# First modulation panels as TensorE's moving operand, slices dealt to four column groups, input loaded first, one block fewer

## The chip, the cores and the metric

The kernel runs on one core of one Trainium2 chip. The metric is the device time of one execution in microseconds, the median of the runs. Three runs of the kernel before gave 1554.28, 1550.50 and 1553.59 us, median 1553.59. The profile is of one further execution of 1552.17 us; the span that it shows, from the first to the last instruction, is 1550.4 us. TensorE is called PE in the rows, VectorE DVE, ScalarE ACT, GpSimd POOL, and SyncE, which starts the DMAs, SP.

## The reference, cut to what matters

Two transformer-like blocks run on 512 tokens of width 1024 in float32. Each starts from a modulation vector, a matrix-vector product; the change touches only the first one, its bias and the first norm behind it:

```python
c_act = jax.nn.silu(c)                        # c: 1 x 1024
mod = c_act @ ada_w[i] + ada_b[i]             # ada_w: 1024 x 6144
sh1, sc1, g1, sh2, sc2, g2 = split(mod, 6)
h = rms_norm(x, mix_pre_g[i]) * (1.0 + sc1) + sh1
y = hybrid_mixer(h, w_in[i], ...)             # projections, attention, 31-tap convolution
x = x + g1 * rms_norm(y, mix_post_g[i])
```

The first projection needs h, so it needs `sh1` and `sc1` in full, 2048 of the 6144 columns. `g1` (1024 columns) is needed only behind the mixer.

## The kernel before

Everything lies transposed: 128 partitions hold features, the free dimension holds the 512 tokens, and a tensor of width 1024 is KT = 8 such tiles. Weights come in panels of 1 MB (128 x 2048), loaded by SP into two `raw` slots. ScalarE rounds a panel to `whi` (`split_hi`, line 187), VectorE forms the rest `wlo` (`split_lo`, line 191), and TensorE makes three passes, `whi` with `hhi`, `whi` with `hlo`, `wlo` with `hhi`. `in_panel` (line 242) is 48 matmuls of 512 columns. TensorE, VectorE and ScalarE each work through a hand-written order; semaphores join them. SP loads panel c+2 once `lo_split` says that the slot is free.

**Modulation panels.** The modulation matrix is also cut into panels of 1 MB: panel c holds 1024 rows as eight slices of 128 partitions (index k) by 256 output columns. Panels 0 to 7 (ADA_OWN = 8) are `sh1` and `sc1`, panels 8 to 11 are `g1`. `first` has room for panels 0 to 7, `ada_raw` holds two more at a time.

**First block, lines 544 to 646.** SP loads the vectors, the constants, modulation panel 0, the input `x` (2 MB), modulation panels 1 to 6 with weight panel 0 behind the last, modulation panel 7, weight panel 1, modulation panels 8 and 9, and then, each behind a wait, modulation panels 10 and 11 and weight panels 2 and 3. Panels 0 to 9 are multiplied and summed off TensorE, by turns (string `BY`, line 528). For even c GpSimd multiplies the panel by the activated vector `cs` (line 586) and VectorE reduces over k (line 609); for odd c VectorE alone runs a chain of eight instructions (lines 615 and 619). TensorE then only sums over the partitions: per panel two matmuls with the 128x128 piece of `ada_acc` as weights and one column of ones as moving operand (line 642; line 215 for panels 8 and 9). The norm of x sits between: squares by ScalarE (line 573, three buffers), sums over the partitions by eight 512-column float32 matmuls with ones as weights (line 638), square root and reciprocal on 128x512. VectorE ends with `split_lo` for weight panels 0 and 1.

**Second block, lines 648 to 663.** `read_mod` (line 234) adds the bias, `coefs` (line 415) forms the factor, and then per tile k VectorE forms `h0` (line 430), ScalarE `hhi` (line 439), VectorE `hlo` (line 424), and TensorE runs the six matmuls of tile k of weight panel 0 (line 449). A block ends when all engines have ended in it.

**Third block, lines 739 on.** TensorE runs weight panels 1 to 6 (`in_panel`, after panel 2 also `small_projection`), VectorE and ScalarE take each result, and VectorE fills its time with the taps of the convolution (line 732; `DENSE_TAPS`, 11 after most panels). Then attention runs in 16 units n: `logits(n)` (lines 790 to 797) on TensorE, maximum (line 1104) on VectorE, exponential (line 1001) on ScalarE, with pieces of later projections between (line 843). `logits(0)` waits for `ncx` (line 1077 on VectorE), `logits(1)` for the exponential of unit 0. Before `logits(0)` and `logits(1)` stands `ada_direct` (line 219): modulation panels 10 and 11 multiplied on TensorE with the panel as weights, 16 float32 matmuls each with one moving column. GpSimd sums modulation panels 12 to 19 after the last tap.

**Helpers that the change newly uses.** `token_sums` (line 292) sums squares with four matmuls of 32 weight columns, each writing its own 32 partitions of one bank for its own 128 tokens; `token_std` and `token_rs` are the root and the reciprocal on 128x128; `spread` (line 312) brings the result back to 128x512 with four matmuls.

## Time and profile before

| what | value |
|---|---|
| median of the runs | 1553.59 us (1550.50 to 1554.28) |
| profiled execution, span | 1552.17 us, 1550.4 us |
| TensorE matmuls busy | 1390.1 us, 90% of the span |
| VectorE busy | 938.6 us, 61% |
| ScalarE, GpSimd busy | 549.5 us, 556.6 us |
| DMA | 181.04 MB, mean 117 GB/s |
| 0 to 60 us: TensorE, VectorE busy | 17.97 us, 44.18 us |
| 80 to 200 us: TensorE, VectorE busy | 115.92 us of 120, 100.58 us |

Times of rows are microseconds from the start of the span unless marked ns. A timeline row gives start, duration, engine, line, operation, output and inputs with shape, how many instructions were merged, and in brackets the idle time of the engine before it with what ended it. A float32 matmul shows as two records, and each record lasts longer than the step to the next one, since matmuls are pipelined. A wait for several semaphores is put down to the one that came last.

### The profile page before, as it was taken

How to read it: one execution, taken by the hardware profiler on the slowest of the kernel's cores; microseconds unless marked ns; L12 is line 12 of the kernel's file. 1: busy time of each engine (PE TensorE's matmuls, PEld its weight loads, DVE VectorE, ACT ScalarE, POOL GpSimd, SP SyncE). 2: the span in 40 equal slices, each digit the busy share in tenths (PEclk: the TensorE clock that was granted, in tenths of full speed). 3: DMA queues.
4: the chain of work that ended last, by engine and by line, in shares of the span. 5: the costliest groups of instructions: out<-in, count | busy, mean ns of one | idle time of the engine just before them, and what ended most of it. 6: DMA issues, size and time to landing. Idle time of an engine off the chain costs nothing. (4 is left out here: it accounts for less than half of the span.)

```text
span 1550.4 us, 18593 instructions
## 1 busy us (share of the span) xinstructions
PE 1390.1 (90%) x7392; PEld 1102.5 (71%) x7392; DVE 938.6 (61%) x1031; ACT 549.5 (35%) x697; POOL 556.6 (36%) x260
## 2 busy tenths in 40 slices
PE   3399987888999998999899979988699899999997
PEld 1378765667888887888678856765478689777775
DVE  6988775776656464323765646777893561355553
ACT  3122345533232222112354433344442342355541
POOL 3000004954987875999200003322300041122320
PEclk8599798988999999999699989999699899999998
DMA  9322211431454545454122233222313243111121
GB/s 389 114 82 77 87 55 58 155 118 77 171 210 173 205 157 195 163 189 190 55 112 90 100 97 109 93 86 70 120 39 104 104 162 109 55 55 55 55 82 55
DMA packets 41346, 181.04 MB, mean 117 GB/s; under 512 B 3392, under 2 KB 20160, under 8 KB 21312
## 3 DMA queue, kind: packets, MB, share of 16 engines
q1 hardware_dynamic: 41280, 180.12, 32.1%
q8 instruction: 46, 0.75, 0.2%
q14 instruction: 20, 0.16, 0.0%
HBM read 173.75 MB, written 6.36 MB: 116 GB/s over the span
## 5 line engine op out<-in xcount | busy, mean ns | idle before, releaser
L191 DVE TENSOR_TENSOR wlo<-raw,whi 128x2048 fp32r<-128x2048 f32 x95 | 264.5, 2785 | 180.9 <-ACT whi L187 178.1
L198 POOL TENSOR_TENSOR ada_raw<-ada_raw,cs 128x2048 f32<-128x2048 f32 x44 | 174.0, 3956 | 380.2 <-DVE cv L732 170.3
L253 PE MATMUL ps<-hhi,whi 128*128 128x512 f32 x640 | 251.8, 393 | 2.4 <-DVE wlo L191 0.8
L253 PE MATMUL ps<-hhi,wlo 128*128 128x512 f32 x640 | 249.4, 390 | 0.0
L253 PE MATMUL ps<-hlo,whi 128*128 128x512 f32 x640 | 249.1, 389 | 0.0
L187 ACT ACTIVATE whi<-raw 128x2048 fp32r<-128x2048 f32 x95 | 181.5, 1911 | 160.1 <-PE ps L1259 94.3
L207 POOL TENSOR_TENSOR ada_raw<-ada_raw 128x1024 f32<-128x1024 f32 x88 | 204.6, 2325 | 6.9
L1732 POOL TENSOR_TENSOR dec<-dec,cb 128x512 f32<-128x512 f32 x32 | 60.8, 1900 | 299.2 <-ACT dec L1698 299.2
L253 PEld LDWEIGHTS ps<-hhi,whi 128*128 128x128 f32 x640 | 120.2, 188 | 28.4 <-issue 2.8
L253 PEld LDWEIGHTS ps<-hhi,wlo 128*128 128x128 f32 x640 | 120.1, 188 | 25.7
L253 PEld LDWEIGHTS ps<-hlo,whi 128*128 128x128 f32 x640 | 120.2, 188 | 24.4
L1924 POOL TENSOR_TENSOR x<-x,rest 128x256 f32<-128x256 f32 (+3 forms) x32 | 49.0, 1532 | 163.3 <-DVE rest L2219 163.3
L2219 DVE TENSOR_TENSOR_SCAN rest<-rest,zero 128x128 f32<-128x128 f32 (+3 forms) x64 | 59.0, 963 | 53.9 <-ACT rest L2139 53.9
L732 DVE SCALAR_TENSOR_TENSOR cv<-u,vec,cv 128x512 f32<-128x512 f32 x120 | 81.8, 744 | 0.4
L1190 DVE TENSOR_TENSOR fg<-ps,fg 128x512 f32<-128x512 f32 x22 | 15.2, 692 | 101.5 <-ACT fg L1180 101.5
L1259 PE MATMUL ps<-fhi,whi 128*128 (+1 forms) x176 | 70.2, 399 | 5.4 <-PEq L1164 5.4
L1180 ACT ACTIVATE fg<-ps 128x512 f32<-128x512 f32 x22 | 13.2, 599 | 174.4 <-PE ps L253 174.4
L1353 DVE SCALAR_TENSOR_TENSOR xbc<-ps,vec,xbc 128x511 f32 (+5 forms) x72 | 48.7, 742 | 42.2 <-ACT xbc L1322 41.8
L1259 PE MATMUL ps<-fhi,wlo 128*128 (+1 forms) x176 | 70.3, 399 | 0.0
L1259 PE MATMUL ps<-flo,whi 128*128 (+1 forms) x176 | 70.1, 399 | 0.0
L1508 PE MATMUL ps<-hhi,whi 128*128 128x512 f32 x128 | 55.9, 437 | 0.0
L1508 PE MATMUL ps<-hlo,whi 128*128 128x512 f32 x128 | 52.0, 407 | 0.0
(368 smaller groups left out, 2939.5 us busy)
## 6 DMA issues: line engine op xcount, KB each, us to landing
raw<-panels SPq DMA_DIRECT2D x95, 1024.0 KB, 4.8
ada_raw<-ada SPq DMA_DIRECT2D x48, 1024.0 KB, 6.6
first<-ada SPq DMA_DIRECT2D x8, 1024.0 KB, 18.5
bc<-ac_rows SPq DMA_DIRECT2D x32, 256.0 KB, 4.4
x_kept<-x SPq DMA_DIRECT2D x2, 2048.0 KB, 9.2
x<-x_kept SPq DMA_DIRECT2D x2, 2048.0 KB, 8.5
x<-x_in SPq DMA_DIRECT2D x1, 2048.0 KB, 12.2
out<-y SPq DMA_DIRECT2D x8, 256.0 KB, 2.2
```

The source lines that it names most:

```text
L187: e.activation(whi[:, c % 2, :, :], raw[:, c % 2, :, :], ACT.Copy).then_inc(hi_split, 1)
L191: e.tensor_tensor(wlo[:, c % 2, :, :], raw[:, c % 2, :, :], whi[:, c % 2, :, :].bitcast(F32), ALU.subtract).then_inc(lo_split, 1)
L198: e.tensor_tensor(ada_raw[:, c % 2, :, :], ada_raw[:, c % 2, :, :], cs[:, which, :].unsqueeze(2).to_broadcast([P, KT, 256]), ALU.mult).the ...
L207: e.tensor_tensor((ada_acc[:, c % 2, :] if sums is None else sums).unsqueeze(1) if width == 1 else part, part, ada_raw[:, c % 2, width:2 * ...
L253: mm = e.matmul(ps[:, 2 * (qc % 2) + b, :], w[:, c % 2, 2 * k + b, :], src[part][:, k, :], **flags)
L732: dve.scalar_tensor_tensor(out=cv[:, j, :], in0=src, scalar=w, in1=cv[:, j, :], op0=ALU.mult, op1=ALU.add).then_inc(A["tap"], 1)
L1259: mm = pe.matmul(ps[:, b, :], w[:, c % 2, k2 * 8 + b, :], src[:, kt, :] if isinstance(i, int) else src[:, bass.ds(kt + i * 4, 1), :], star ...
L1353: ins = dve.scalar_tensor_tensor(out=xbc[:, bass.ds(t, 1), s:S], in0=ps[:, 2 * pair + b, 0:S - s], scalar=vec[:, bass.ds(wc, 1)], in1=xbc[ ...
L1508: mm = pe.matmul(ps[:, 2 * (qp % 2) + b, :], wt[:, cp % 2, 2 * kt + b, :], (hhi, hlo)[part][:, kt, :], start=(kt == 0 and j == 0), stop=(k ...
L1732: pool.tensor_tensor(dec[:, n % 2, :, :], dec[:, n % 2, :, :], cb[:, b // 2, :].unsqueeze(1).to_broadcast([P, HB, P]), ALU.mult).then_inc( ...
L1924: pool.tensor_tensor(sig[:, n % 3, :, 0:nk], sig[:, n % 3, :, 0:nk], rest[:, n % 2, :, S - nk + 1:S + 1], ALU.mult).then_inc(B["am"], 1)
L2219: scan = dve.tensor_tensor_scan(turned, turned, zero[:, 0:1].to_broadcast([P, nk]), 1.0, ALU.mult, ALU.add)
```

## The change

- Modulation panels 0 to 7 go over TensorE. `ada_rows` takes `cs` slice k, one column repeated to 32, as weights and the panel's slice k (128x256, float32) as moving operand; slice k = 2g + half writes partitions 32g to 32g+31 of a bank. So four slices go to four groups of 32 array columns, twice. `ada_keep` with a copy brings the 128x256 result to `ada_acc`, on VectorE in the first block. `ada_turn` makes columns of it with two matmuls against `quad`, a vector with 1 at partitions 0, 32, 64 and 96. GpSimd has no work in the first block.
- Panels 8 to 11 go the same way inside the third block: rows of 8 and 9 behind weight panel 3, their turn behind panel 4, rows of 10 and 11 behind panel 5, their turn behind panel 6, the copies on ScalarE. `ada_direct` is gone. SP loads panels 10 and 11 between weight panels 6 and 7.
- `x` is loaded ahead of modulation panel 0, weight panel 0 behind modulation panel 5. All eight squares have a buffer of their own; sums, root, reciprocal and `spread` use the helpers, the sums behind the rows of panel 1 and `spread` behind those of panel 2.
- The norm and weight panel 0's matmuls stand in the first block, and the second block is gone. `split_lo` of weight panel 0 stands behind the copy of panel 5, that of weight panel 1 behind the norm.

```diff
+        quad = sbuf(ctx, "quad", [P, 1])
...
-        def ada_direct(e, c):
-
-            e.wait_ge(ada_landed[c % 2], (c // 2 + 1 - ADA_OWN // 2) * 16)
+        def ada_rows(pe, c, src, bank):
+
             which = 0 if c < ADA_C2 else 1
+            if c >= 2:
+                pe.wait_ge(rows_kept, c - 1)
+            for half in range(2):
+                for g in range(TB):
+                    k = 2 * g + half
+                    mm = pe.matmul(ps[32 * g:32 * g + 32, bank, 0:256], cs[:, which, k:k + 1].to_broadcast([P, 32]),
+                                   src[:, k, :], start=half == 0, stop=half == 1, skip_group_check=True)
+            mm.then_inc(rows_done, 1)
+
+        def ada_keep(e, c, bank):
+
+            e.wait_ge(rows_done, c + 1)
+            if c >= 2:
+                e.wait_ge(mod_done, c - 1)
+            return ada_acc[:, c % 2, :], ps[:, bank, 0:256]
+
+        def ada_turn(pe, c):
+
+            pe.wait_ge(rows_kept, c + 1)
             for b in range(2):
-                for k in range(KT):
-                    mm = e.matmul(ps[:, MODB, 2 * c + b:2 * c + b + 1], ada_raw[:, c % 2, k, b * P:(b + 1) * P],
-                                  cs[:, which, k:k + 1], start=k == 0, stop=k == KT - 1)
+                mm = pe.matmul(ps[:, MODB, 2 * c + b:2 * c + b + 1], ada_acc[:, c % 2, b * P:(b + 1) * P], quad[:],
+                               start=True, stop=True)
             mm.then_inc(mod_done, 1)
-            e.sem_inc(acc_ready, 1)
...
-        read_counts = {(0, ADA_FIRST): 1, (10, 12): 2, (12, 20): 3, (20, 41): 4, (41, 54): 5, (54, 56): 6}
+        read_counts = {(0, ADA_OWN): 1, (8, 12): 2, (12, 20): 3, (20, 41): 4, (41, 54): 5, (54, 56): 6}
...
-            xsq = sbuf(seg, "xsq", [P, 3, S])
-            rs0 = sbuf(seg, "rs0", [P, S])
-
-            BY = "PDPDPDPDPD"
-            first_mul = sem("first_mul")
-            first_acc = sem("first_acc")
+            xsq = sbuf(seg, "xsq", [P, KT, S])
+            h0 = sbuf(seg, "h0", [P, 2, S])
             first_landed = [sem(f"first_landed{c}") for c in range(ADA_OWN)]
...
             x_landed = sem("x_landed")
...
+            x0 = counting(sq_ready=KT, ss_used=KT, std_ready=1, rs_ready=1, spread=1)
+            head = pre_norm(v("mix_pre"), "sc1", "sh1", hhi, hlo, h0, ps[:, 7, :])
             with nc.Block() as block:
                 @block.sync
                 def _(sp):
                     sp.dma_start(vec[:], vecs).then_inc(setup, 16)
                     sp.dma_start(consts[:].rearrange("p a b -> p (a b)"), cst).then_inc(setup, 16)
+                    sp.dma_start(x[:], x_in).then_inc(x_landed, 16)
                     for c in range(ADA_OWN):
                         sp.dma_start(first[:, c, :, :].rearrange("p k n -> p (k n)"),
                                      ada[c]).then_inc(first_landed[c], 16)
-                        if c == 0:
-                            sp.dma_start(x[:], x_in).then_inc(x_landed, 16)
-                        if c >= ADA_OWN - 2:
-                            load_panel(sp, c - ADA_OWN + 2, 0)
+                        if c == ADA_OWN - 3:
+                            load_panel(sp, 0, 0)
+                    load_panel(sp, 1, 0)
                     for c in range(2):
                         load_ada(sp, ADA_OWN + c, 0)
-                    for c in range(2):
-                        load_ada(sp, ADA_FIRST + c, 0)
                     for c in range(2, 4):
                         load_panel(sp, c, 0)
...
                     for k in range(KT):
-                        if k >= 3:
-                            act.wait_ge(xss, k - 2)
-                        act.activation(xsq[:, k % 3, :], x[:, k, :], ACT.Square).then_inc(xsq_ready, 1)
-                    act.wait_ge(xss, KT)
+                        act.activation(xsq[:, k, :], x[:, k, :], ACT.Square).then_inc(nsem["sq_ready"], 1)
                     act.wait_ge(pair_free[0], 1)
-                    act.activation(rs0[:], ps[:, 0, :], ACT.Sqrt, bias=eps[:, 0:1], scale=1.0 / D).then_inc(x_std, 1)
+                    token_std(act, x0, 0, 7)
                     split_hi(act, 0, 0)
                     split_hi(act, 1, 0)
...
-
-                @block.gpsimd
-                def _(pool):
-                    pool.wait_ge(ada_chain, 1)
-                    for c in range(ADA_FIRST):
-                        if BY[c] == "P":
-                            pool.wait_ge(*landed(c))
-                            pool.tensor_tensor(landing(c), landing(c),
-                                               cs[:, 0, :].unsqueeze(2).to_broadcast([P, KT, 256]),
-                                               ALU.mult).then_inc(first_mul, 1)
+                    head["act"](act)
...
-                    dve.sem_inc(acc_ready, ADA_OWN)
-                    dve.wait_ge(ada_chain, 1)
-                    n = 1
-                    slot_user = {}
-                    for c in range(ADA_FIRST):
-                        if c == 3:
-                            dve.wait_ge(x_std, 1)
-                            dve.reciprocal(rs0[:], rs0[:]).then_inc(x_rs, 1)
-                        src = landing(c)
-                        counted = first_acc if c < ADA_OWN else acc_ready
-                        if c % 2 in slot_user:
-                            dve.wait_ge(mod_done, slot_user[c % 2] + 1)
-                        slot_user[c % 2] = c
-                        if BY[c] == "P":
-                            dve.wait_ge(first_mul, BY[:c + 1].count("P"))
-                            dve.tensor_reduce(ada_acc[:, c % 2, :], src.rearrange("p k n -> p n k"),
-                                              AX.X, ALU.add).then_inc(counted, 1)
-                            continue
-                        dve.wait_ge(*landed(c))
...
-                            else:
-                                dve.wait_ge(ada_chain, n)
-                                ins = dve.scalar_tensor_tensor(out=ada_acc[:, c % 2, :], in0=src[:, k, :],
-                                                               scalar=cs[:, 0, k:k + 1], in1=ada_acc[:, c % 2, :],
-                                                               op0=ALU.mult, op1=ALU.add)
...
-                                ins.then_inc(counted, 1)
-                    split_lo(dve, 0, 0)
+                    dve.sem_inc(acc_ready, ADA_POOL)
+                    dve.wait_ge(setup, 32)
+                    dve.tensor_reduce(quad[:], ident[:, 0:P:32], AX.X, ALU.add).then_inc(ada_chain, 1)
+                    for c in range(ADA_OWN):
+                        if c == 2:
+                            token_rs(dve, x0, 0)
+                        kept, rows = ada_keep(dve, c, 2 + c % 2)
+                        dve.tensor_copy(kept, rows).then_inc(rows_kept, 1)
+                        if c == ADA_OWN - 3:
+                            split_lo(dve, 0, 0)
+                    read_mod(dve, 0, ADA_OWN)
+                    dve.wait_ge(mod_read, read_counts[(0, ADA_OWN)])
+                    head["coefs"](dve)
+                    dve.wait_ge(x_landed, 16)
+                    dve.wait_ge(*x0("spread", 1))
+                    head["dve"](dve)
                     split_lo(dve, 1, 0)
 
                 @block.tensor
                 def _(pe):
-                    pe.wait_ge(ada_chain, 1)
+                    pe.wait_ge(ada_chain, 2)
                     pe.wait_ge(setup, 32)
                     for c in range(ADA_OWN):
-                        if c == 0:
+                        pe.wait_ge(first_landed[c], 16)
+                        ada_rows(pe, c, first[:, c, :, :], 2 + c % 2)
+                        if c == 1:
                             for k in range(KT):
-                                pe.wait_ge(xsq_ready, k + 1)
-                                pe.matmul(ps[:, 0, :], ones, xsq[:, k % 3, :], start=k == 0,
-                                          stop=k == KT - 1).then_inc(xss, 1)
-                        pe.wait_ge(first_acc, c + 1)
-                        for b in range(2):
-                            mm = pe.matmul(ps[:, MODB, 2 * c + b:2 * c + b + 1],
-                                           ada_acc[:, c % 2, b * P:(b + 1) * P], ones[:, 0:1], start=True, stop=True)
...
-                    for c in range(ADA_OWN, ADA_FIRST):
-                        ada_columns(pe, c, 0)
...
-            head = pre_norm(v("mix_pre"), "sc1", "sh1", hhi, hlo, xsq, rs0[:])
-            with nc.Block() as block:
-                @block.scalar
-                def _(act):
-                    head["act"](act)
-
-                @block.tensor
-                def _(pe):
+                                token_sums(pe, x0, 0, k, xsq, 7)
+                        if c == 2:
+                            spread(pe, x0, 0, 7)
+                        if c:
+                            ada_turn(pe, c - 1)
+                    ada_turn(pe, ADA_OWN - 1)
                     head["pe"](pe, 0, 0)
-
...
-                        order = ["w4", "w5", "w6", "w7", "w8", "w9", "w10", "a12", "a13", "w11", "w12", "a14", "w13", "a15",
+                        order = ["w4", "w5", "w6", "a10", "a11", "w7", "w8", "w9", "w10", "a12", "a13", "w11", "w12", "a14", "w13", "a15",
                                  "a16", "a17", "a18", "w14", "a19", "a20", "w15", "a21", "w16", "w17"]
...
-                                    sp.wait_ge(mod_done, j - 1)
+                                    sp.wait_ge(rows_done, j - 1)
...
-                        for r in range(2, 10):
-                            ada_reduce(pool, a0 + r, 0, macc[:, r - 2, :])
+                        for a in range(12, 20):
+                            ada_reduce(pool, a, 0, macc[:, a - 12, :])
...
+                            for a in {3: (8, 9), 5: (10, 11)}.get(c, ()):
+                                pe.wait_ge(ada_landed[a % 2], (a // 2 + 1 - ADA_OWN // 2) * 16)
+                                ada_rows(pe, a, ada_raw[:, a % 2, :, :], 6 + a % 2)
+                            for a in {4: (8, 9), 6: (10, 11)}.get(c, ()):
+                                ada_turn(pe, a)
...
                         m = 0
                         for n in range(NU + 3):
-                            if n < 2:
-                                ada_direct(pe, a0 + n)
...
                             split_hi(act, s + 2, 0)
+                            for a in {3: (8, 9), 5: (10, 11)}.get(s, ()):
+                                kept, rows = ada_keep(act, a, 6 + a % 2)
+                                act.activation(kept, rows, ACT.Copy).then_inc(rows_kept, 1)
...
```

## Rows read from the trace of the kernel before

**Rows 1.** The page, 40 slices of 38.8 us: TensorE's busy tenths.
```profile
PE   3399987888999998999899979988699899999997
```

**Rows 2.** Busy time by stretch: us, PE, PEld, DVE, ACT, POOL, clock, DMA.
```profile
42.00:58.00 16.00, 3.46 (x14) 3.20 (x15) 15.46 (x20) 0.00 (x0) 0.81 (x1) 0.50 0.00 0
```

**Rows 3.** Timeline, all engines: what the loads ended.
```profile
14.32 1.67 ACT L573 ACTIVATE xsq<-x 128x512 f32<-128x512 f32 x3 [9.26 <-DMA x<-x_in]
31.70 1.91 ACT L187 ACTIVATE whi<-raw 128x2048 fp32r<-128x2048 f32 x1 [5.79 <-DMA raw<-panels]
36.68 1.91 ACT L187 ACTIVATE whi<-raw 128x2048 fp32r<-128x2048 f32 x1 [3.06 <-DMA raw<-panels]
```

**Rows 4.** Timeline: end of the first block, start of the norm.
```profile
61.35 4.49 DVE L191 TENSOR_TENSOR wlo<-raw,whi 128x2048 fp32r<-128x2048 f32 x2
61.48 1.01 PE L215 MATMUL ps<-consts,ada_acc 128*128 128x1 f32 x4 [2.89 <-DVE ada_acc L619]
66.64 0.18 DVE L234 TENSOR_TENSOR mod<-ps,vec 128x20 f32<-128x20 f32 x1 [0.80 <-PEq L544]
67.05 1.42 DVE L430 SCALAR_TENSOR_TENSOR xsq<-x,coef,rs 128x512 f32<-128x512 f32 x2
69.49 0.77 PE L449 MATMUL ps<-hhi,whi 128*128 128x512 f32 x1 [7.00 <-DVE hlo L424]
```

**Rows 5.** Timeline: end of the norm, start of weight panel 1.
```profile
77.30 1.63 DVE L424 SCALAR_TENSOR_TENSOR hlo<-xsq,mod,hhi 128x512 fp32r<-128x512 f32 x2
82.44 0.47 PE L253 MATMUL ps<-hhi,whi 128*128 128x512 f32 x1 [0.47 <-PEq L649]
```

**Rows 6.** Timeline: full-width float32 matmuls of the first block, at the higher clock.
```profile
22.88 0.19 PEld L638 LDWEIGHTS ps<-xsq,consts 128*128 128x128 f32 x1 [0.24 <-issue]
25.02 0.95 PE L642 MATMUL ps<-consts,ada_acc 128*128 128x1 f32 x8
```

**Rows 7.** Timeline of PE: `token_sums` behind the output projection, at either clock.
```profile
322.77 0.40 PE L861 MATMUL ps<-hlo,whi 128*128 128x512 f32 x1
323.01 0.39 PE L861 MATMUL ps<-hhi,wlo 128*128 128x512 f32 x1
323.33 0.43 PE L296 MATMUL ps<-pm,consts 128*32 128x128 f32 x8
323.68 0.50 PE L861 MATMUL ps<-hhi,whi 128*128 128x512 f32 x1
...
337.91 0.65 PE L296 MATMUL ps<-pm,consts 128*32 128x128 f32 x8 [2.95 <-ACT pm L373]
338.49 1.01 PE L349 MATMUL ps<-consts,macc 128*128 128x1 f32 x4
```

**Rows 8.** Busy time by stretch: the last part of that alternation.
```profile
346.00:348.00 2.00, 2.00 (x18) 1.48 (x14) 1.34 (x1) 0.00 (x0) 0.00 (x0) 0.50 0.00 0
```

**Rows 9.** Timeline, all engines: third block around weight panels 3 to 6.
```profile
121.62 0.69 DVE L1042 TENSOR_TENSOR u<-ps,pt 128x512 f32<-128x512 f32 x1 [4.89 <-ACT pt L943]
...
132.79 1.91 ACT L187 ACTIVATE whi<-raw 128x2048 fp32r<-128x2048 f32 x1
134.73 2.29 DVE L191 TENSOR_TENSOR wlo<-raw,whi 128x2048 fp32r<-128x2048 f32 x1
...
154.06 3.63 PE L225 MATMUL ps<-cs,ada_raw 128*128 128x1 f32 x32
155.18 1.90 ACT L187 ACTIVATE whi<-raw 128x2048 fp32r<-128x2048 f32 x1
159.35 2.29 DVE L191 TENSOR_TENSOR wlo<-raw,whi 128x2048 fp32r<-128x2048 f32 x1
159.57 0.58 PE L790 MATMUL ps<-k1hi,q1hi 64*128 64x256 f32 x2 [1.88 <-DVE ncx L1077]
```

**Rows 10.** Timeline, all engines: the first attention unit.
```profile
169.30 0.37 ACT L1001 ACTIVATE pm<-ps,nmx 128x128 f32<-128x128 f32 x1 [12.22 <-DVE nmx L1104]
170.16 0.58 PE L790 MATMUL ps<-k1hi,q1hi 64*128 64x256 f32 x2
```

More of the change, by code:

```diff
@@ L161, in build @@
         sg_ready = sem("sg_ready")
+        rows_done = sem("rows_done")
+        rows_kept = sem("rows_kept")
         small_landed = sem("small_landed")
@@ L524, in build @@
             first = sbuf(seg, "first", [P, ADA_OWN, KT, 256])
-            xsq = sbuf(seg, "xsq", [P, 3, S])
-            rs0 = sbuf(seg, "rs0", [P, S])
-            BY = "PDPDPDPDPD"
-            first_mul = sem("first_mul")
-            first_acc = sem("first_acc")
+            xsq = sbuf(seg, "xsq", [P, KT, S])
+            h0 = sbuf(seg, "h0", [P, 2, S])
             first_landed = [sem(f"first_landed{c}") for c in range(ADA_OWN)]
             x_landed = sem("x_landed")
-            def landing(c):
-                return first[:, c, :, :] if c < ADA_OWN else ada_raw[:, c % 2, :, :]
-            def landed(c):
-                return (first_landed[c], 16) if c < ADA_OWN else (ada_landed[c % 2], 16)
-            xsq_ready = sem("xsq_ready")
-            xss = sem("xss")
-            x_std = sem("x_std")
-            x_rs = sem("x_rs")
+            x0 = counting(sq_ready=KT, ss_used=KT, std_ready=1, rs_ready=1, spread=1)
+            head = pre_norm(v("mix_pre"), "sc1", "sh1", hhi, hlo, h0, ps[:, 7, :])
             with nc.Block() as block:
@@ L699, in build @@
                 pad_ready = sem("pad_ready")
-                a0, w0 = ADA_FIRST, FIRST["wo"]
+                w0 = FIRST["wo"]
                 DENSE = 7
@@ L1111, in _ @@
                             if n == 11:
-                                read_mod(dve, 10, 12)
+                                read_mod(dve, 8, 12)
                             if n == 12:
-                                dve.wait_ge(mod_read, read_counts[(10, 12)])
+                                dve.wait_ge(mod_read, read_counts[(8, 12)])
                                 post1["coefs"](dve)
```

18 lines of the change are left out of this document (1 added, 17 removed).

## The prediction

> **What bounds the kernel now.** I read first TensorE's tenths on the page [rows 1]. They stand at 8 or 9 over most of the span, but the first two slices, 78 us, are at 3: there TensorE waits, and the change lies there. Next the stretch 42 to 58 us [rows 2]: the loads are silent (0 GB/s), TensorE is busy 3.46 us, VectorE 15.46 of 16. So the first block is bound by VectorE's sums over modulation panels, not by DMA. The timeline gives the loads [rows 3]: x has landed by 14.32, weight panel 0 by 31.70, weight panel 1 by 36.68. Between x and weight panel 0 lie seven loads of 1 MB, so one takes (31.70 - 14.32)/7 = 2.48 us, and modulation panel 7, between the weight panels, is there at 31.70 + 2.48 = 34.2. But its columns, with 8's and 9's behind, are finished only at 62.5 (61.48 + 1.01), the norm starts at 67.05 and TensorE's real work at 69.49 [rows 4]. Some 28 us are to be had.
>
> In the third block I follow two engines [rows 9]. TensorE runs its panels without a gap, and VectorE, once it has waited 4.89 us for panel 3's gate at 121.62, is never early by much: `logits(0)` waits 1.88 us for it at 159.57, and the first exponential waits for a maximum that stands behind eleven taps, so `logits(1)` starts only at 170.16 [rows 10]. What is added on TensorE before that can move VectorE's chain.
>
> **Price of one panel's rows.** A float32 matmul over the full array has two records; at the higher clock one record follows another after 0.19 + 0.24 = 0.43 us at 512 columns [rows 6], so a matmul costs 0.86, at the lower clock double. Eight matmuls of 256 columns, one after another, would cost 8 x 0.43 = 3.4 us, or 6.9 at the lower clock. That is the upper bound. The nearest rows for column groups are those of `token_sums`, four matmuls of 128 columns in four groups [rows 7]. One after another they would cost 4 x 0.215 = 0.86 us and 1.71 at the lower clock; the next instruction starts after 0.35 (323.33 to 323.68) and 0.58 (337.91 to 338.49). So the groups run beside one another. The step between the clocks, 0.23 us, is column time, and the fixed part is 0.12. `ada_rows` has four times the columns: 4 x 0.23 + 0.12 = 1.04 us at the higher clock, 4 x 0.46 + 0.12 = 1.96 at the lower. I take 1.0 and 2.0, since shape and form are the same.
>
> A turn is two full matmuls with one moving column: 0.95/2 = 0.48 us at the higher clock [rows 6], 1.01 at the lower [rows 7]. The copy between is one 128x256 instruction. It finishes beside the previous panel's turn, so it costs nothing while that turn lasts about as long.
>
> The Trainium skill, in "TensorEngine Tiling (Array Packing)", Key Properties, speaks against this change: changing the tiling mode drains TensorE, and each panel changes it twice. The row beside it: the call before 323.33 is reached 0.32 us after the start of the matmul ahead of it, where the step between two of those is 0.24 (322.77 to 323.01), 0.08 more [rows 7]; going back is inside my 0.12. If each change cost as much as a whole 0.39 us record, the last panel would be about 0.6 us later and the sum with it.
>
> **First block.** SP: the bytes ahead of panel 7 are the same, so it still lands at 34.2; x lands one load earlier, 11.8. Moving x past panel 0 delays panel 0 to 14.3, which nobody uses before that but TensorE. TensorE at the lower clock: rows of panel 0 to 16.3, of panel 1 16.8 to 18.8; eight `token_sums` at 0.58 end at 23.4 and a turn at 24.4 while panel 2 has been there since 19.3. It is then behind the loads. In the trace of before TensorE was at 2.4 GHz by 22.88, some 8 us after its full-width sums over the squares had begun, and was back at 1.2 GHz after work with gaps (a matmul of one column takes 0.24 us at 25.02 and 0.5 at 61.48 [rows 3, 4, 6]). I take it to rise during the sums, at about 21, to catch up by panel 5 or 6 (1.5 us of work per panel of 2.48), and to be at 1.2 GHz again for the last two. `spread`, four full matmuls of 128 columns (0.86 us of columns at 2.4 GHz, 1.71 at 1.2, say 1.2 and 2.0), lies in the backlog.
>
> The last panel then: landed 34.2, rows to 36.2, turn of 6 to 37.2, turn of 7 to 38.2. The bias, the coefficient and the step to `h0` take 0.41 us (66.64 to 67.05 [rows 4]), signals 0.2: `h0` starts at 38.8 instead of 67.05, **28.2 us earlier**. Gone are GpSimd's products, VectorE's sums, panels 8 and 9 and one block's end (0.80 us [rows 4]), all inside that difference. What is late next is the last load, then TensorE's two turns. ScalarE's `split_hi` of weight panel 1, which now stands ahead of its part of the norm, runs 36.7 to 38.6 and the first `hhi` is asked for at 39.6: covered by 1 us; were it not, each us late is a us lost.
>
> The norm keeps its pace, and TensorE's matmuls of weight panel 0 start 2.44 us after `h0`, as 67.05 to 69.49. VectorE's last `hlo` ends at 78.93 - 28.2 = 50.7 [rows 5]. The moved `split_lo` (4.49/2 = 2.25 us [rows 4]) ends at 52.9, and only then does SP issue weight panel 3, which it used to do long before. The block end costs 0.80 from VectorE's end [rows 4], so 53.7; TensorE's last matmul (81.96, 0.48 ahead of the start at 82.44 [rows 5]) ends at 53.7 too, and the third block starts at about 54.2. The same 28.2, with the move hidden by a hair; a bound for it is 1 us. Weight panel 3 is used 12 us later. But the small `w_f` load queues behind it, and VectorE waits for that ahead of nearly everything: about one load, 2.5 us, later than now. The 4.89 us of waiting at 121.62 [rows 9] covers it.
>
> **Third block.** Counted in the old times. Rows of 8 and 9 behind panel 3: two at 1.0, panel 4 ends 2.0 later. Turns, 0.95: panel 5 ends 2.9 later. Rows of 10 and 11: panel 6 ends 4.9 later, at 154.06 + 4.9 = 159.0, its turns at 159.9. Two chains go from there. Panel 4: its `whi` (132.79, to 134.70) moves by 2.0, and VectorE, which took it at 134.73 without a gap, moves by 2.0 [rows 9]; so does `ncx`, and `logits(0)` starts at 161.5. Panel 6: `whi` ends at 155.18 + 1.90 + 4.9 = 162.0, while VectorE, which was there at 159.35 with 2.3 us in hand, now comes at 161.4 and waits for it. Its eleven taps, the maximum, the exponential and `logits(1)` are thus **2.6 us later**. The removed `ada_direct` (3.63 us at 154.06 and as much again ahead of `logits(1)`) gives nothing back: the first makes room for the rows, the second stood in TensorE's wait for the exponential. ScalarE's four copies, under 1 us a pair, lie in its waits. SP's loads of panels 10 and 11 hold up weight panel 7 until the rows of 9 are done, at 123, yet its slot comes free only after 125. GpSimd's sums start with the last tap, as before. Nothing behind that point changes its order.
>
> **Sum.** 1552.17 - 28.2 + 2.6 = 1526.6 us for the profiled execution. The median of the runs is 1.4 above it, so 1528.0.
>
> **Rivals.** (a) The lower clock all through the first block. For it: while TensorE alternated `token_sums` with turns from 338 on it was busy 2.00 of 2.00 us and the granted clock stayed 0.50 [rows 8]. Against: that mix streams columns for a third of its time, rows for most. Price: from 24.4 on, rows, `spread` and turns cost 2.0 + 2.0 + 1.0 for panel 2 and 3.0 for each of panels 3 to 7, and the last turn ends at 45.4 instead of 38.2. Some of that is given back, nothing is added: about 1534.
>
> (b) The reverse, the higher clock also for panels 6 and 7: rows to 35.2, turns to 36.3, 1.9 us better, 1526. It lies within the forecast's range.
>
> (c) No overlap between the groups at 256 moving columns, the change not doing what it says. For it only the lack of a row of that size, against it both pairs in [rows 7]. At the higher clock 3.4 + 0.5 us per panel: 14.3 + 8 x 3.9 + 4.6 + 1.2 + 3 for the slow start = 54.3, norm at 54.9, 12.1 gained; the third block loses 4 x 3.4 + 0.95 - 2.3 = 12.3. Result 1554, no change.
>
> (d) Slower: the same serial groups with the lower clock in the first block, 6.9 + 1.0 us per panel. The last turn ends at 14.3 + 63.2 + 4.6 + 2.0 = 84.1, norm at 84.7, 17.6 later than now, and the third block loses 12.3: 1583. It turns slower from a panel price of (67.05 - 12.3 - 0.6 - 20.9)/8 = 4.2 us.
>
> (e) The third block gives back more than 2.6: the clock falls behind each pair of rows and the next panel begins at 1.2 GHz, which for some 3 us costs 1.5 to 2 each time, or a load or `w_f` comes too late for the 4.89. Two such losses and more: 1534 to 1541.
>
> **Chances.** The forecast 68%, its own range 1522 to 1531 (the clock of the last panels, 0.2 us on each price, and the 3.8 us over which the runs spread); (a) 17%, (c) 5%, (d) 5%, (e) 5%. Range: 1522 to 1538, which takes in (a) and half of (e). A measurement of this kernel tells 0.3% or 4.7 us from no change. Faster by more: forecast, (a) and (e), 0.90; within 0.3%: (c), 0.05; slower: (d), 0.05.
>
> **What would show it.** In the profile after: `ada_rows` of the last panels with the next instruction 1.0 or 2.0 us behind its start, not 3.4; the last turn at 36 to 39 us; `h0` at 37 to 39; weight panel 1 from about 54; `logits(0)` waiting for `ncx`; `logits(1)` 2.6 us further from the third block's start than now (170.16 - 82.44 = 87.7, so 90.4). The prediction fails if the 256-column rows don't overlap, if TensorE never leaves 1.2 GHz before 40 us, or if the distance from the third block's start to the end grows by much more than 2.6.

## The result and the profile after

The changed kernel takes 1528.61 us (median of 4 runs, 1527.08 to 1530.34) against 1552.37 us of the kernel before in the same comparison; the ratio is 0.9848, 95% interval 0.9832 to 0.9865. The forecast was 1528.0 us. The profiled execution took 1527.57 us, with a span of 1525.8 us.

The timeline of the changed kernel, from the loads to the norm. The rows of the last two panels answer to [rows 4], the loads to [rows 3]:

```profile
9.52 4.27 ACT L574 ACTIVATE xsq<-x 128x512 f32<-128x512 f32 x8 [4.17 <-DMA x<-x_in]
12.13 1.94 PE L229 MATMUL ps<-first,cs 128*32 128x256 f32 x16 [12.13 <-DMA first<-ada]
...
16.23 2.25 PE L314 MATMUL ps<-xsq,consts 128*32 128x128 f32 x64
...
22.74 1.07 PE L229 MATMUL ps<-first,cs 128*32 128x256 f32 x16
23.74 0.61 PE L244 MATMUL ps<-quad,ada_acc 128*128 128x1 f32 x4
...
27.00 0.61 PE L244 MATMUL ps<-quad,ada_acc 128*128 128x1 f32 x4
30.97 1.94 PE L229 MATMUL ps<-first,cs 128*32 128x256 f32 x16 [3.37 <-DMA first<-ada]
33.78 1.93 PE L229 MATMUL ps<-first,cs 128*32 128x256 f32 x16
35.64 1.87 PE L244 MATMUL ps<-quad,ada_acc 128*128 128x1 f32 x8
35.92 1.91 ACT L189 ACTIVATE whi<-raw 128x2048 fp32r<-128x2048 f32 x1 [5.55 <-DMA raw<-panels]
37.55 0.17 DVE L252 TENSOR_TENSOR mod<-ps,vec 128x16 f32<-128x16 f32 x1 [1.34 <-PE ps L244]
38.06 1.41 DVE L448 SCALAR_TENSOR_TENSOR h<-x,coef,ps 128x512 f32<-128x512 f32 x2
38.85 1.38 ACT L457 ACTIVATE hhi<-h,mod 128x512 fp32r<-128x512 f32 x2 [1.01 <-DVE h L448]
40.50 0.76 PE L467 MATMUL ps<-hhi,whi 128*128 128x512 f32 x1 [2.99 <-DVE hlo L442]
```

The sixteen records of one panel's rows take 1.0 us to the next instruction at 2.4 GHz (22.74 to 23.74) and 1.86 at 1.2 GHz (33.78 to 35.64). The first block follows the loads now: TensorE waits 3.37 us for panel 6 at 30.97. `h0` starts at 38.06 where it was 67.05.

The level of the clock before the first rise is read from these steps. The profile's clock column (third from the end in busy rows) stands at 1.00 from the start of the span, also at 12 to 14 us, where a panel's rows take 1.94 us. The rise shows in how many records of `token_sums` fall into 0.8 us:

```profile
16.00:16.80 0.80, 0.80 (x20) 0.54 (x13) 0.28 (x1) 0.00 (x0) 0.00 (x0) 1.00 0.96 399
17.10:17.90 0.80, 0.80 (x40) 0.80 (x36) 0.00 (x0) 0.00 (x0) 0.00 (x0) 1.00 1.03 430
```

TensorE came to 2.4 GHz at about 16.9 us, during the sums over the squares.

The third block, its start and the rows that answer to [rows 5, 9, 10]:

```profile
53.88 0.47 PE L271 MATMUL ps<-hhi,whi 128*128 128x512 f32 x1 [0.47 <-PEq L549]
57.29 0.27 DVE L482 MEMSET wf_hi<- 128x256 f32 x1 [2.81 <-DMA wf_raw<-w_f]
...
92.28 1.93 PE L229 MATMUL ps<-ada_raw,cs 128*32 128x256 f32 x32
93.02 0.69 DVE L1003 TENSOR_TENSOR u<-ps,pt 128x512 f32<-128x512 f32 x1 [3.41 <-ACT pt L901]
105.16 0.94 PE L244 MATMUL ps<-quad,ada_acc 128*128 128x1 f32 x8
106.41 1.23 DVE L1010 SCALAR_TENSOR_TENSOR q1lo<-ps,q1hi 128x1024 fp32r<-128x1024 f32 x1 [1.38 <-ACT q1hi L903]
108.22 2.29 DVE L193 TENSOR_TENSOR wlo<-raw,whi 128x2048 fp32r<-128x2048 f32 x1 [0.58 <-ACT whi L189]
133.06 0.58 PE L750 MATMUL ps<-k1hi,q1hi 64*128 64x256 f32 x2 [1.56 <-DVE ncx L1038]
133.61 2.29 DVE L193 TENSOR_TENSOR wlo<-raw,whi 128x2048 fp32r<-128x2048 f32 x1 [0.80 <-ACT whi L189]
144.42 0.58 PE L750 MATMUL ps<-k1hi,q1hi 64*128 64x256 f32 x2 [4.39 <-ACT pm L962]
```

Three new waits of VectorE stand there, 1.38 and 0.58 us behind weight panel 4 and 0.80 behind panel 6. Together they are 2.76 us. `logits(1)` starts 144.42 - 53.88 = 90.54 us after the block, 2.8 us more than before.

| kernel | `h0` starts | third block starts | `logits(1)` behind it | end of span behind it | median, us |
|---|---|---|---|---|---|
| before | 67.05 | 82.44 | 87.72 | 1467.96 | 1552.37 |
| changed | 38.06 | 53.88 | 90.54 | 1471.92 | 1528.61 |
| e10_changed_again | 38.52 | 55.43 | 90.53 | 1473.17 | 1530.50 |
| e1_full_width | 52.46 | 69.29 | 100.25 | 1483.21 | 1553.40 |
| e2_warm | 36.27 | 51.97 | 90.54 | 1471.63 | 1526.25 |
| e3_no_gate_rows | 38.84 | 54.58 | 87.68 | 1468.42 | 1526.60 |
| e4_rows_later | 39.12 | 55.90 | 87.67 | 1469.60 | 1526.69 |
| e5_warm_later | 36.20 | 54.09 | 87.68 | 1469.21 | 1523.87 |
| e6_x_second | 37.57 | 54.95 | 90.54 | 1472.85 | 1528.09 |
| e7_two_blocks | 42.26 | 59.05 | 90.54 | 1476.95 | 1533.62 |
| e8_w3_in_third | 37.18 | 52.42 | 87.68 | 1468.98 | 1524.76 |
| e9_quarters | 37.48 | 51.99 | 87.68 | 1468.21 | 1523.31 |

The first four columns of numbers are from each kernel's one profiled execution. The third of them repeats to 0.01 us; the first two move by about 1 and 2 us between kernels with the same first block, so small effects there have to be read step by step.

### The profile page after: what moved, and what is told of

Its sections match the earlier page's. It is cut to its first block and busy times, and to the rows that moved or that the text cites. A ratio compares the mean times of both kernels' runs of the same rounds, so it can differ in the third digit from the quotient of the medians.

```text
span 1525.8 us, 18940 instructions
## 1 busy us (share of the span) xinstructions
PE 1392.9 (91%) x7584; PEld 1097.3 (72%) x7584; DVE 892.6 (58%) x995; ACT 550.2 (36%) x701; POOL 538.0 (35%) x255
## 5 line engine op out<-in xcount | busy, mean ns | idle before, releaser
L209 POOL TENSOR_TENSOR ada_raw<-ada_raw 128x1024 f32<-128x1024 f32 x88 | 200.5, 2279 | 6.9
L1141 ACT ACTIVATE fg<-ps 128x512 f32<-128x512 f32 x22 | 13.2, 599 | 174.3 <-PE ps L271 174.3
L1151 DVE TENSOR_TENSOR fg<-ps,fg 128x512 f32<-128x512 f32 x22 | 15.2, 692 | 101.1 <-ACT fg L1141 101.1
## 6 DMA issues: line engine op xcount, KB each, us to landing
first<-ada SPq DMA_DIRECT2D x8, 1024.0 KB, 16.9
```

Of the source, the lines that this page charges most:

```text
L209: e.tensor_tensor((ada_acc[:, c % 2, :] if sums is None else sums).unsqueeze(1) if width == 1 else part, part, ada_raw[:, c % 2, width:2 * ...
```

## The experiments

**Do the column groups carry the gain? e1_full_width**

```diff
-            for half in range(2):
-                for g in range(TB):
-                    k = 2 * g + half
-                    mm = pe.matmul(ps[32 * g:32 * g + 32, bank, 0:256], cs[...].to_broadcast([P, 32]), ...
+            for k in range(KT):
+                mm = pe.matmul(ps[:, bank, 0:256], cs[:, which, k:k + 1].to_broadcast([P, P]), src[:, k, :],
+                               start=k == 0, stop=k == KT - 1)
...
-                    dve.tensor_reduce(quad[:], ident[:, 0:P:32], AX.X, ALU.add)
+                    dve.tensor_copy(quad[:], ident[:, 0:1])
```

> Rows of a modulation panel as eight accumulating matmuls with 128 equal weight columns over the whole array instead of four groups of 32; everything else as in the changed kernel. If the four column groups are what makes the rows cheap, a panel's rows cost 3.4 us at 2.4 GHz (6.9 at 1.2) where the changed kernel has 1.0 (1.9). TensorE is then the bound of the first block: h0 starts near 49 instead of 38, each pair of rows in the third block costs 6.8 instead of 1.9, and logits(1) starts 100 us after the third block's start instead of 90.5. Time about 1549 us. If it was taking the sums off VectorE alone, and the groups don't matter, h0 stays at 38 and the time near 1529.

Measured: 1553.40 us, ratio to the kernel before 1.0002 (0.9990 to 1.0014). The timeline of TensorE in the first block:

```profile
14.83 9.58 PE L227 MATMUL ps<-first,cs 128*128 128x256 f32 x32 [14.83 <-DMA first<-ada]
...
31.48 3.70 PE L227 MATMUL ps<-first,cs 128*128 128x256 f32 x16
35.02 0.50 PE L242 MATMUL ps<-quad,ada_acc 128*128 128x1 f32 x4
```

A panel's rows cost 3.54 us (31.48 to 35.02) instead of 1.0, and `logits(1)` comes 100.25 us after the third block's start. With the sums on TensorE over the whole array, nothing is left of the gain. The first block still gains: `h0` starts 14.6 us earlier than in the kernel before and the third block 13.2. But from there to the end of the span it takes 15.3 us more (1483.21 against 1467.96), 12.5 of them up to `logits(1)`, where the rows of panels 8 to 11 now stand. Whole-array sums in the first block alone, with panels 8 to 11 done elsewhere, were not run. The time is that of rival (c), 1554. My 1549 was 4 us low: `h0` came at 52.5, not 49. The first panel landed at 14.83 here, 2.7 us later than in the changed kernel's profile, which is most of the difference.

**Is the clock of the first block worth anything? e2_warm**

```diff
+                    def warm_up(n):
+                        for _ in range(n):
+                            pe.matmul(ps[:, 6, :], ones, xsq[:, 0, :], start=True, stop=True)
...
+                        if c == 5:
+                            warm_up(3)
                     ada_turn(pe, ADA_OWN - 1)
+                    warm_up(2)
                     head["pe"](pe, 0, 0)
```

> Adds five full-width float32 matmuls of 512 columns into an unused bank: three behind the turn of panel 4, two behind the last turn. If the gap of TensorE at 27.6 to 31 us is what brings 1.2 GHz back for the last two panels and the first part of the norm, the clock stays at 2.4 GHz from 16 us on, the last two rows cost 1.0 instead of 1.9 and their turns 0.5 instead of 1.0, h0 starts at about 36.5 instead of 38.1, the norm's matmuls take 11 instead of 12.9 us, and the third block starts near 52 instead of 53.9: 1526.7 us. If the clock of the first block isn't worth anything (loads or ScalarE's rounding of weight panel 1, which ends at 37.8, are the bound), h0 moves by less than 0.5 and the time stays within 0.5 of the changed kernel.

Measured: 1526.25 us, 0.9830 (0.9806 to 0.9854), `h0` at 36.27, third block at 51.97. The busy rows of both kernels in the same stretches (us, PE, PEld, DVE, ACT, POOL, granted clock, DMA, GB/s), first the changed kernel, then e2_warm:

```profile
30.00:32.00 2.00, 1.03 (x12) 0.58 (x16) 1.60 (x1) 0.37 (x1) 0.00 (x0) 0.64 0.98 410
42.00:44.00 2.00, 2.00 (x6) 1.57 (x5) 1.97 (x4) 0.72 (x1) 0.00 (x0) 0.50 0.04 16
```

```profile
30.00:32.00 2.00, 2.00 (x18) 0.73 (x18) 1.58 (x1) 0.38 (x1) 0.00 (x0) 1.00 1.02 426
42.00:44.00 2.00, 2.00 (x10) 1.35 (x9) 1.93 (x4) 0.97 (x2) 0.00 (x0) 1.00 0.11 45
```

Five matmuls whose result nobody reads keep TensorE at 2.4 GHz and bring `h0` 1.8 us and the third block 1.9 us forward. The first theory holds, to 0.2 us for both. In the changed kernel's profile the gap at 27.6 to 31 us, TensorE's wait for a load, is what cost the clock: with the gap filled it didn't fall. The medians alone would not show it clearly; the runs of the two kernels overlap (1525.40 to 1527.83 against 1527.08 to 1530.34).

**Where does the third block lose? e3_no_gate_rows and e4_rows_later**

e3 leaves the rows, copies and turns of panels 8 to 11 out, so the gate `g1` isn't computed:

```diff
...
-                                ada_rows(pe, a, ada_raw[:, a % 2, :, :], 6 + a % 2)
+                                pe.sem_inc(rows_done, 1)
...
-                                ada_turn(pe, a)
+                                pe.sem_inc(mod_done, 1)
...
```

> Leaves out the rows, copies and turns of modulation panels 8 to 11 in the third block (the gate g1 is then twice its bias and the output is not the reference's); semaphores are counted on. By the two chains of the prediction this gives back 2.6 us: logits(1) starts 87.9 us after the third block's start instead of 90.5, time about 1526.0. If all of TensorE's added 5.7 us lay on the path, the distance falls to 84.8 and the time to 1523. If VectorE's chain covered it, the distance stays at 90.5 and so does the time.

Measured: 1526.60 us, `logits(1)` 87.68 us after the block's start.

e4 does the same work in other places. ScalarE's copies move with it, and weight panel 7 is loaded ahead of modulation panels 10 and 11:

```diff
...
-                            for a in {3: (8, 9), 5: (10, 11)}.get(c, ()):
+                            for a in {4: (8, 9)}.get(c, ()):
                                 ...
                                 ada_rows(pe, a, ada_raw[:, a % 2, :, :], 6 + a % 2)
-                            for a in {4: (8, 9), 6: (10, 11)}.get(c, ()):
+                        for a in (8, 9):
                                 ada_turn(pe, a)
+                        for a in (10, 11):
+                            ...
+                            ada_rows(pe, a, ada_raw[:, a % 2, :, :], 6 + a % 2)
...
+                            if n == 1:
+                                for a in (10, 11):
+                                    ada_turn(pe, a)
                             if n < NU:
                                 logits(n)
...
```

> Same work, other places: rows of panels 8 and 9 behind weight panel 4 (not 3), their turns behind weight panel 6, the rows of 10 and 11 behind these, and the turns of 10 and 11 in TensorE's wait ahead of logits(1); weight panel 7 is loaded ahead of modulation panels 10 and 11. If the loss comes by the two chains named (panel 4's end to ncx, panel 6's end to the rounding of weight panel 8), panel 4 ends as early as in the kernel before, panel 6 only 1.9 later, within VectorE's 2.3 us in hand, and logits(1) comes 87.9 us after the third block's start: 1526.0 us. If it is TensorE's total work that counts, it stays at 90.5 and 1528.6.

Measured: 1526.69 us, `logits(1)` 87.67 us after the block's start. Both bring the distance back to that of the kernel before, 87.72. TensorE's 5.7 us of added work (twice 1.93 and twice 0.94) cost 2.8, and none up to `logits(1)` when it stands where VectorE is the later one. The distance shows this, not the medians, which lie only 2.0 and 1.9 us under the changed kernel's. In e4's timeline of TensorE, the rows of panels 10 and 11 fill the wait ahead of `logits(0)`; the last of them are shown, and 0.61 us of the wait are still left:

```profile
131.76 0.61 PE L229 MATMUL ps<-ada_raw,cs 128*32 128x256 f32 x8
132.99 0.39 PE L753 MATMUL ps<-k1hi,q1hi 64*128 64x256 f32 x2 [0.61 <-DVE ncx L1044]
```

Its third block starts 2.0 us later than the changed kernel's, with nothing changed ahead of it. The loads landed 1.4 us later (ScalarE took weight panel 1 at 37.30, not 35.92), and the norm ran more of its time at 1.2 GHz, as a busy row of e4 shows (columns as above; the changed kernel has 1.00 there):

```profile
46.00:48.00 2.00, 2.00 (x8) 1.57 (x7) 1.97 (x4) 0.72 (x1) 0.00 (x0) 0.67 0.00 0
```

**How much of that is spread? e10_changed_again**, the changed kernel unaltered.

> The changed kernel once more, unaltered, on this chip, for the spread of its first block between executions: 1528.6 us; h0 at 38 to 39.5 and third block at 53.5 to 56 depending on when the loads land and when TensorE's clock rises in the norm, logits(1) 90.5 us behind it whatever these are. If the first block were as fixed as the third, h0 would be at 38.1 and the third block at 53.9 again.

Measured: 1530.50 us (1529.09 to 1531.14), third block at 55.43, `logits(1)` 90.53 behind it. So 1.5 us between two executions lie ahead of the third block alone, and the third block's first 90 us don't move at all. The two medians of one kernel, 1528.61 and 1530.50, are 1.9 us apart, too; differences of medians below that are not told from nothing here.

**Input first: e6_x_second**

```diff
-                    sp.dma_start(x[:], x_in).then_inc(x_landed, 16)
                     for c in range(ADA_OWN):
                         sp.dma_start(first[:, c, :, :]..., ada[c]).then_inc(first_landed[c], 16)
+                        if c == 0:
+                            sp.dma_start(x[:], x_in).then_inc(x_landed, 16)
```

> The changed kernel with x loaded behind modulation panel 0, as in the kernel before. Panel 7 lands at the same time whatever the order, and TensorE has caught up with the loads by then, so h0 stays at 38 to 39 and the time at 1528.6. If loading the input first is part of the gain, because the sums over the squares start later and TensorE doesn't catch up, h0 comes up to 2.5 us later: 1531.

Measured: 1528.09 us, `h0` at 37.57. The sums over the squares end later (22.6 instead of 18.4), and TensorE catches up with the loads only at panel 7. Loading x first is worth nothing by itself in the medians. The two profiles reach the same `h0` by different ways, though. In e6 the loads landed 1.3 us later (ScalarE took weight panel 1 at 37.25, not 35.92). But TensorE, being behind, had no wait ahead of panel 6 and ran panels 6 and 7 at 2.4 GHz, their rows in 1.0 us, which the changed kernel's profile has at 1.86.

```profile
10.07 1.94 PE L229 MATMUL ps<-first,cs 128*32 128x256 f32 x16 [10.07 <-DMA first<-ada]
17.38 1.93 PE L229 MATMUL ps<-first,cs 128*32 128x256 f32 x16 [5.37 <-DMA first<-ada]
19.08 3.53 PE L314 MATMUL ps<-xsq,consts 128*32 128x128 f32 x64
...
34.79 1.07 PE L229 MATMUL ps<-first,cs 128*32 128x256 f32 x16
35.79 1.22 PE L244 MATMUL ps<-quad,ada_acc 128*128 128x1 f32 x8
```

**One block fewer: e7_two_blocks**

```diff
                     split_hi(act, 1, 0)
-                    head["act"](act)
...
-                    read_mod(dve, 0, ADA_OWN)
-                    ...
-                    head["dve"](dve)
                     split_lo(dve, 1, 0)
...
+            with nc.Block() as block:
+                @block.scalar
+                def _(act):
+                    head["act"](act)
...
+                @block.vector
+                def _(dve):
+                    read_mod(dve, 0, ADA_OWN)
+                    ...
+                    head["dve"](dve)
```

> The changed kernel with the norm and weight panel 0's matmuls in a second block again, and the rounding of weight panel 1 (split_lo) ahead of it, as in the kernel before. The block's end then waits for ScalarE's rounding of panel 1 (until 37.8), VectorE's 2.3 us behind it, the issue of weight panel 3 and 0.8 us: h0 at 41.3 instead of 38.1, third block 3.3 us later, time 1531.9 us. If only the block's end itself costs, it is 0.8 us: 1529.4.

Measured: 1533.62 us, 0.9875 (0.9859 to 0.9890), `h0` at 42.26.

```profile
36.70 1.91 ACT L189 ACTIVATE whi<-raw 128x2048 fp32r<-128x2048 f32 x1 [5.55 <-DMA raw<-panels]
38.65 2.29 DVE L193 TENSOR_TENSOR wlo<-raw,whi 128x2048 fp32r<-128x2048 f32 x1 [1.98 <-ACT whi L189]
40.97 0.33 SPq L175 DMA_DIRECT2D raw<-panels  x1
41.74 0.17 DVE L252 TENSOR_TENSOR mod<-ps,vec 128x16 f32<-128x16 f32 x1 [0.80 <-PEq L549]
42.26 1.41 DVE L448 SCALAR_TENSOR_TENSOR h<-x,coef,ps 128x512 f32<-128x512 f32 x2
```

The chain is the expected one. Against e10_changed_again, where weight panel 1 landed at the same time (its rounding starts at 36.69), `h0` is 3.7 us later and the third block 3.6. The merging is a real part of the gain, and only 0.8 of it is the block's end; the rest is what had to be done ahead of that end. The profiled execution, 1537.76 us, is the slowest of its four, but the median, too, lies 3 to 5 us over the two medians of the changed kernel.

**Both improvements: e5_warm_later, e8_w3_in_third, e9_quarters.** e5 is e2's and e4's edits together.

> The five added matmuls of e2_warm and the places of e4_rows_later together. If the two losses lie in different stages and don't share a cover, they add up: third block at 52.0 as in e2_warm, logits(1) 87.7 us behind it as in e4_rows_later, time 1526.25 - 2.4 = 1523.9 us. If they share something (the clock at the start of the third block, VectorE's backlog), it stays near 1526.

Measured: 1523.87 us, 0.9816 (0.9803 to 0.9830), as summed. Yet its profile has the third block at 54.09, not 52.0:

```profile
36.20 1.41 DVE L448 SCALAR_TENSOR_TENSOR h<-x,coef,ps 128x512 f32<-128x512 f32 x2
37.41 1.91 ACT L189 ACTIVATE whi<-raw 128x2048 fp32r<-128x2048 f32 x1 [7.08 <-DMA raw<-panels]
39.22 1.32 ACT L457 ACTIVATE hhi<-h,mod 128x512 fp32r<-128x512 f32 x2
39.96 0.75 DVE L442 SCALAR_TENSOR_TENSOR hlo<-h,mod,hhi 128x512 fp32r<-128x512 f32 x1 [2.35 <-ACT hhi L457]
40.86 0.47 PE L467 MATMUL ps<-hhi,whi 128*128 128x512 f32 x1 [3.39 <-DVE hlo L442]
```

ScalarE's rounding of weight panel 1 is no longer covered: it stands in front of the first `hhi` and holds the norm up 2.35 us, and TensorE falls back to 1.2 GHz behind its wait. Not all of this comes from the earlier `h0`. e2 has the same first block and the same `h0` (36.27), but there the rounding started at 35.95 and held VectorE up only 0.83 us, the clock stayed up, and the third block started at 51.97. So 0.8 us are due to the earlier `h0`, and 1.5 to a load that came later in this one execution, which at 1525.08 us is the slowest of e5's five. e8 issues weight panel 3 in the third block:

```diff
-                    for c in range(2, 4):
-                        load_panel(sp, c, 0)
+                    load_panel(sp, 2, 0)
...
                         sp.dma_start(wf_raw..., w_f).then_inc(small_landed, 16)
+                        load_panel(sp, 3, 0)
```

> e5_warm_later with the load of weight panel 3 issued in the third block behind the small w_f load, instead of at the first block's end. VectorE's last instruction then ends the first block alone: third block 0.3 us earlier relative to h0 than in e5_warm_later, and VectorE's wait for w_f falls from 2 to 3 us to about 1. The latter is covered by its wait at panel 3's gate and gives nothing: 1523.6 us. If the wait for w_f did cost, 1521 to 1522.

Measured: 1524.76 us (1523.02 to 1528.25), no difference from e5 that the runs can tell. VectorE's wait for `w_f` fell from 3.08 to 1.07 us and `logits(1)` stayed at 87.68: that wait is covered. e9 cuts the rounding into pieces:

```diff
-                    split_hi(act, 1, 0)
-                    head["act"](act)
+                    for k in range(KT):
+                        head["act"](act, k, k + 1)
+                        if 1 <= k < 5:
+                            act.wait_ge(w_landed[1], 16)
+                            part = slice(4 * k - 4, 4 * k)
+                            ins = act.activation(whi[:, 1, part, :], raw[:, 1, part, :], ACT.Copy)
+                            if k == 4:
+                                ins.then_inc(hi_split, 1)
```

> e8_w3_in_third with ScalarE's rounding of weight panel 1 cut into four pieces of 128x512, one behind each hhi of tiles 1 to 4, where ScalarE has 0.72 us free per tile, instead of whole and ahead of all. In e5_warm_later and e8_w3_in_third the whole piece stood in front of the first hhi (2.35 and 0.84 us of VectorE's waiting). If that is what kept the gain of the earlier h0 down, the first hhi follows h0 by 0.8 us, TensorE's gap ahead of the norm shrinks to about 1 us so the clock stays at 2.4 GHz, and the third block starts 14.7 us after h0 instead of 15.2 (e8) and 17.9 (e5), at 51 us: 1522.5 us. If weight panel 1's load is the bound itself, or the pieces hold up the hhi's, no gain: 1524 to 1525.

Measured: 1523.31 us, 0.9819 (0.9805 to 0.9832). The third block starts 14.5 us after `h0`, against 15.2 in e8 (and 17.9 in e5 with its late load); the gap of TensorE is 1.17 us:

```profile
38.26 1.38 ACT L457 ACTIVATE hhi<-h,mod 128x512 fp32r<-128x512 f32 x2 [6.66 <-DVE h L448]
39.01 0.75 DVE L442 SCALAR_TENSOR_TENSOR hlo<-h,mod,hhi 128x512 fp32r<-128x512 f32 x1
39.54 0.61 ACT L582 ACTIVATE whi<-raw 128x512 fp32r<-128x512 f32 x1
39.91 0.47 PE L467 MATMUL ps<-hhi,whi 128*128 128x512 f32 x1 [1.17 <-DVE hlo L442]
```

The mechanism is shown in the trace; as a time, e5, e8 and e9 are the same within their runs. Their medians lie 3.9 to 5.3 us under the changed kernel's 1528.61, and further under e10's 1530.50; only e8's slowest run, 1528.25, reaches into the changed kernel's.

## Why the prediction was right, step by step

**What bounds the kernel**: right. The first block followed VectorE's sums and follows the loads now.

**Price of the rows**: right. 1.04 and 1.96 us were worked out from `token_sums`, 1.0 and 1.86 were measured, and e1's 3.54 against my 3.4 shows that the upper bound was well placed. The doubt from the Trainium skill ("TensorEngine Tiling (Array Packing)", Key Properties), that changing the tiling mode drains TensorE, would have shown as some 0.6 us a panel over my price; the panel came out under it. The Trainium skill's "TensorE: Matmul & The Clock Gate", Part 3, gives 2.38 times for three column tiles at 512 columns; four groups at 256 columns measured 3.54 / 1.0 = 3.5 times here.

**First block**: the sum was right (28.2 forecast, 28.6 in the profile, 27.0 in e10's), the terms were off both ways, and that they nearly cancel is luck. x had landed at 9.5, not 11.8 (10.9 in e10), and weight panel 1 at 35.9, not 36.7. TensorE's clock rose at 16.9, not 21, within the sums over the squares, which took 2.2 us for eight (3.0 in e10) instead of the 4.6 that I priced at 1.2 GHz. It was back at the lower level for panels 6 and 7, as assumed (in e10 for panel 7 only), so `h0` came at 38.06 against 38.8. The norm's matmuls then took 12.9 us (40.50 to 53.41), not 12.5, since 1.2 GHz lasted to about 44; in e4 and e10 they took 13.9 and 14.0 (41.56 to 55.43 and 40.95 to 54.96). That term, "the norm keeps its pace", was mis-sized by 0.4 to 1.5 us.

**The covers**: each of the three named held. ScalarE's rounding left 1.01 us ahead of the first `hhi` (1 forecast), and e2, with 0.83 us of waiting, and e5, with 2.35, showed what happens when it isn't covered. The `split_lo` and the issue of weight panel 3 behind the norm ended beside TensorE. VectorE's longer wait for `w_f` (2.81 us) was taken out of the 4.89 at panel 3's gate, of which 3.41 were left; e8 confirms it.

**Third block**: right in size and cause. `logits(1)` moved 2.8 us, 2.6 forecast, by the two chains named: 1.38 + 0.58 = 1.96 us behind panel 4 (2.0 forecast) and 0.80 more behind panel 6 (0.6). e3 and e4 each take it away. (87.7 + 2.6 is 90.3, not the 90.4 that stands under "What would show it".)

**The sum**: closer than its terms. For the profiled execution 1526.6 was forecast and 1527.57 measured: 28.56 us gained ahead of the third block, 3.96 lost behind it, where 28.2 and 2.6 were forecast. The gain was forecast as 25.6 us and measured as 23.8 between the medians, 21.4 in e10's comparison. The time of 1528.0 was met to 0.6 us because the median of the kernel before also came out lower in the comparison, 1552.37 and not 1553.59.

**What is left open**: from the third block's start to the end the changed kernel takes 3.96 us more in its profile (5.2 in e10's), of which the 2.8 are explained. Kernels that are the same from there on (changed, e2, e6, e7, e10) spread from 1471.6 to 1477.0. The prediction put everything behind `logits(1)` at nothing; it isn't. The traces place part of it. Counted from the third block's start, the changed kernel is 2.8 us later than the kernel before at `logits(1)`, 1.3 at one of ScalarE's later roundings of a weight panel (602.60 us; 629.86 before), 3.2 at the rounding nine panels on (703.40; 728.74), 4.65 at ScalarE's table load that begins a later block (757.28; 781.19) and 4.0 at the end. Between the second and the third of these points the roundings lie 11.20 us apart instead of 10.99, nine times over, in e9 and e10 as well. Between the third and the fourth the granted clock is 0.50 from 720 to 747 us, 27 us, where the kernel before had it for 24 us (748 to 772). Why the panels take 0.21 us more each, and why the clock stays down longer, is open.

**The rivals**: (c) was the time of the kernel without column groups, 1554 against 1553.4 measured in e1. (a) did not come: the clock rose early. (b) was real money, yet had to be paid for with extra matmuls: e2 is (b) and keeps the norm at 2.4 GHz besides, 1526 forecast, 1526.25 measured, which is closer than two medians of one kernel lie.

## What to carry to other kernels

At 2.4 GHz a matrix-vector product goes over TensorE at the speed of its loads (1.5 us of rows and turn for a load of 2.5) if the vector is the stationary operand, repeated over 32 columns, and the slices go to four column groups; over the whole array the same work costs 3.5 times as much and here, with four of the twelve panels in a stage where TensorE had little to spare, that ate the whole gain. Look for added work's place by asking at each step which engine is late there: the same 5.7 us of TensorE cost 2.8 us or nothing. When a stage gets faster, the piece that was just covered becomes the next bound, so list the covers with their widths beforehand.

## What the runs showed of the hardware

TensorE at 2.4 GHz was at 1.2 GHz again behind a wait of 3.37 us for a load (27.6 to 31.0 in the changed kernel), and likewise in e5 behind its wait of 3.39 us ahead of the norm; behind waits of 1.88 us (e8) and 1.17 us (e9) in the same place it was not. The length of the one wait doesn't decide it, though. In e4 the clock was down behind a wait of 1.91 us ahead of panel 6, and in e6 behind one of 1.29 ahead of `spread`, where the same wait left it up in e4 and e10:

```profile
32.33 1.07 PE L229 MATMUL ps<-first,cs 128*32 128x256 f32 x16 [1.91 <-DMA first<-ada]
34.83 1.93 PE L229 MATMUL ps<-first,cs 128*32 128x256 f32 x16 [0.77 <-DMA first<-ada]
```

```profile
25.44 1.79 PE L334 MATMUL ps<-rsq,consts 128*128 128x128 f32 x8 [1.29 <-DVE rsq L328]
26.00:28.00 2.00, 2.00 (x14) 1.99 (x17) 0.00 (x0) 0.00 (x0) 0.00 (x0) 0.50 1.00 418
```

(The first two rows are e4's, the others e6's.) Narrow matmuls in four column groups did raise the clock: it was up at about 16.9 us, when TensorE had run nothing but two panels' rows and the first of the `token_sums` since 12.1. In the kernel before, `token_sums` alternating with turns had stayed at 1.2 GHz though busy 2.00 of 2.00 us [rows 8]. And the loads that start the kernel land up to 2.9 us apart from one execution to another (the first modulation panel at 12.13 in the changed kernel and 15.02 in e4_rows_later, whose first block is the same).
